# RMSNorm of the next phase inside the input-embedding loop, and a five-slot weight ring, in an eight-core encoder trunk

## The chip, the cores and the metric

The kernel runs on all eight NeuronCores of one Trainium2 chip. Each core computes one of the eight batch elements; the cores exchange nothing. The metric is the device time of the slowest core, in microseconds (us).

A core has five engines that are coupled by semaphores alone: TensorE (PE in the profile) multiplies matrices from SBUF into the eight PSUM banks, VectorE (DVE) and ScalarE (ACT) do elementwise work, GpSimd (POOL) issues DMAs here and little else, SyncE (SP) issues DMAs. Every engine works its own instructions off in program order.

## What is computed

Four layers over a residual stream `h` of 2048 tokens by 1024 channels for each core. Two layers (A) are chunked gated MLPs, two (B) are stick-breaking attention with shared K and V, made once after layer 1.

```python
h = x
for i in range(4):
    hn = rmsnorm(h, norm_g[i])
    if i < 2:
        mix = gmlp_mixer(hn, ...)        # z = hn @ w_in (1024 x 6144); ... @ w_out (2048 x 1024)
    else:
        if k_sh is None:
            kv = rmsnorm(h, kv_norm_g) @ w_kv
        mix = (stick_breaking(q, k_sh, v_sh) * silu(gate)) @ b_w_out[j]   # q, gate = hn @ b_w_in[j]
    h = h + mix
    h = h + sigmoid(h @ ple_gate_w[i]) * (p[i] @ ple_w[i])                # per-layer input embedding
return rmsnorm(h, final_g)
```

The last line of the loop is what the change touches, together with the `rmsnorm` that follows it.

## The kernel before

**Tiling.** `H` (16 tiles of 128 tokens by 1024 channels, float32) stays in SBUF for the whole program. Work goes in halves of 1024 tokens, that is eight tiles: layer 0 half 0, layer 0 half 1, layer 1 half 0, and so on; after layer 1 come two K/V phases (`phase_kv`), one for each half. Every phase needs `HT`, the transposed bfloat16 copy of eight normalized tiles; there is one `HT`, so a half's copy is overwritten by the next one.

**A phase.** `phase_norm` (L423) loads the gain vector into `GB` (L424, queue SP), which is the same memory as `TAA`. Then for each of eight tiles DVE writes `HN` = `H` x `RS` x `GB` (L429), PE transposes it in eight small matmuls (L448) and ACT copies the result to `HT` (L450). The row scales `RS` come from `norm_stats`, which a phase runs ahead for the other half; so they are there before they are needed, with few exceptions. Then the layer's own matmuls run: for A layers L493 (the v columns), the spatial gate L533/L539, L562/L567 (u and gate columns) and the output projection L599 with the residual add L603; for B layers L721 (q and gate), the attention steps, and the output projection L909 with the residual add L913. The output projection has two passes over the eight tiles, one for each half of the output columns (`dc`). In the second pass each tile is also cast to bfloat16 (L437, DVE), transposed (L448) and copied to `HT` (L450): this is the input of the embedding's gate.

**The embedding, `phase_ple`.** Two passes again, `dc` = 0 and 1, each over eight tiles. A tile of a pass is eight gate matmuls (L633), two matmuls of the embedding (L638), a tanh on ACT into `TAA` (L642), and two DVE instructions, L644 and L648, the second of which updates `H`. `HT` is read by both passes. When both are over, the next phase begins with `phase_norm`; its load of `GB` waits until DVE has read `TAA` for the last time.

**The weight ring.** Weights come as units of 128 x 2048 values (read as float32, written as bfloat16, 512 KB each) by DMAs on POOL's queue. `NSLOT` = 4 slots lie in `RING`; A layers have two more in `X`. `ring_begin` marks all earlier units as done (`keep=1` spares one), `ring_next` takes the next unit, `ring_prefetch` issues loads as far as slots are marked free. A load's issue waits on POOL until PE has read the slot's old unit. The embedding has five units: two of gate weights for `dc` = 0 (PW0, PW1), one of embedding weights for both passes (PW2), two of gate weights for `dc` = 1 (PW3, PW4). The output projection of an A layer has eight units (WO0 to WO7), four for each pass; that of a B layer four (BO0 to BO3), two for each pass.

**Order.** The program is recorded by `Sched` as it is written: each engine's order is the order of the calls in the code. `Sched.op` adds the waits that reads and writes of the named regions need.

Of the kernel before, what the change touches and what calls it, by code (L numbers as in the profile page):

```python
# [1 line left out]
OPT = "sp"  # L2
# [5 lines left out]
F32 = mybir.dt.float32  # L8
# [181 lines left out]
VOFF = {}  # L190
# [28 lines left out]
def build(layers=(0, 1, 2, 3), final=True, dbg=False):  # L219
# [63 lines left out]
    SML = sb("SML", [128, 64], F32)  # L283
    ST8 = sb("ST8", [128, 192], F32)
    ST = SML[:, 0:24]
# [27 lines left out]
    rLP = [Reg(), Reg(), Reg()]; rAT = [Reg(), Reg()]  # L313
    rLNG = Reg(); rLNB = Reg(); rVH2 = [Reg(), Reg()]; rWST = Reg(); rBS = Reg(); rBSHL = Reg(); rBSR = Reg()
    rST = Reg(); rMV = Reg(); rSV = Reg()
    rST8 = [Reg() for _ in range(8)]
    rX = [Reg(f"X{i}") for i in range(8)]
    rPS = [Reg(f"ps{i}") for i in range(8)]
    rY = Reg("Y")

    cnt = {"ta": 0, "tb": 0, "hn": 0, "bank": 0, "lp": 0, "at": 0}

# [129 lines left out]
    def phase_A(l, hf):  # L452
# [154 lines left out]
        if l == 0 and hf == 0:  # L607
            dump("H1", H[:, 0:8192], rH[0:8])
        phase_ple(l, hf)

    def phase_ple(l, hf):
        if "p" not in OPT:
            for ii in range(8):
                ple_prep_tile(hf, ii)
        base = widx["PW", l]
        sw = None
        wp = None
        for dc in range(2):
# [70 lines left out]
    def phase_B(l, hf):  # L689
        if True:  # L690
# [209 lines left out]
            for dc in range(2):  # L900
# [3 lines left out]
                for ii in range(8):  # L904
# [74 lines left out]
```

How the kernel before makes its waits and increments, by code:

```python
    def _wait(self, eng, toks):  # L59
        best = {}
        for t in toks:
            if t is None:
                continue
            assert t.sem is not None, f"unresolved token from {t.eng} needed by {eng}"
            key = t.sem
            if key not in best or best[key].val < t.val:
                best[key] = t
        for key, t in best.items():
            if self.seen[eng].get(key, 0) >= t.val:
                continue
            self.E[eng].wait_ge(t.sem, t.val)
            self.seen[eng][key] = t.val
# [23 lines left out]
    def op(self, eng, fn, reads=(), writes=(), signal=True):  # L96
        self._wait(eng, self._deps(eng, reads, writes))
        inst = fn(self.E[eng])
        tok = Tok(eng)
        if signal:
            if self.cnt[eng] >= SEM_CHUNK:
                self._newsem(eng)
            self.cnt[eng] += 1
            inst.then_inc(self.sems[eng], 1)
            tok.sem = self.sems[eng]
            tok.val = self.cnt[eng]
            for p in self.pending[eng]:
                p.sem = tok.sem
                p.val = tok.val
            self.pending[eng] = []
        else:
            self.pending[eng].append(tok)
        self._mark(tok, reads, writes)
        return tok
# [1 line left out]
    def dma(self, q, out, in_, semname, reads=(), writes=()):  # L116
# [3 lines left out]
        ent = self.dsem[semname]  # L120
        ent[1] += 16
        self.E[q].dma_start(out=out, in_=in_).then_inc(ent[0], 16)
        tok = Tok("dma:" + semname)
```

## Time and profile before

| | us |
|---|---|
| median of 3 runs | 3573.12 |
| range of these runs | 3570.70 to 3576.19 |
| the profiled execution, its own time | 3588.44 |
| its span, first to last instruction, slowest core (core 5) | 3587.4 |
| spans of the eight cores | 3553.2 to 3587.4 |

| engine | busy us | share of the span |
|---|---|---|
| PE | 2611.7 | 73% |
| DVE | 1959.7 | 55% |
| ACT | 1747.1 | 49% |
| POOL | 131.1 | 4% |

The shares are of the whole span and hide that the stages have different limits. The places of interest are found in the chain of work that ended last: the profile follows it back from the last instruction, at each step to what released it. A DMA in that chain is time in which the core waited for a transfer. In the timeline a bracket tells how long an engine was idle before an instruction and what released it.

### The profile page before, as it was taken

The page shows a single profiled execution, that of the slowest core. Times are in us where ns is not written, and L with a number is a line of the kernel's source. Part 1 is how long each engine was busy: PE and PEld are TensorE (multiplying, and loading weights), DVE is VectorE, ACT ScalarE, POOL GpSimd, SP SyncE. Part 2 cuts the span into 40 slices and gives each one's busy share as a digit, 9 for nine tenths or more (in the row PEclk, how much of TensorE's full clock was granted, in tenths as well). Part 3 has the DMA queues.
Part 4 walks back from the last instruction along what each step waited for, and adds up shares of the span by engine and source line. Part 5 has one row for each costly group of instructions (what it writes and reads, how often), then busy time and mean ns, then how long its engine had stood idle before and what let it go on. Part 6 is the DMA issues. An engine that isn't in the chain of part 4 may idle for free.

```text
span 3587.4 us, 44009 instructions; the slowest of 8 cores (3553.2 to 3587.4 us)
## 1 busy us (share of the span) xinstructions
PE 2611.7 (73%) x11968; PEld 1142.0 (32%) x11968; DVE 1959.7 (55%) x3224; ACT 1747.1 (49%) x3147; POOL 131.1 (4%) x247
## 2 busy tenths in 40 slices
PE   2789786978698778978877756676667676667671
PEld 1334332433243333434333322222323332222230
DVE  1444246525643455333488457777458845777743
ACT  3442145314531254114266348888446635888832
POOL 0000000000000000000000000000000000000000
PEclk9769986998699888998888979999979897999996
DMA  6214332423133222423311220000221021000022
GB/s 168 47 32 69 54 64 53 76 41 69 36 65 59 59 48 48 77 45 61 53 19 19 36 41 13 13 7 6 36 41 24 13 46 31 13 13 13 1 36 105
DMA packets 43309, 157.10 MB, mean 44 GB/s; under 512 B 4672, under 2 KB 4800, under 8 KB 42560
## 3 DMA queue, kind: packets, MB, share of 16 engines
q0 software_dynamic: 36016, 126.50, 20.7%
q1 hardware_dynamic: 7056, 27.79, 2.2%
q8 instruction: 106, 1.74, 0.2%
q14 instruction: 131, 1.07, 0.1%
HBM read 272.37 MB, written 8.39 MB: 78 GB/s over the span
## 4 chain that ended last, share of the span: by engine, by line
PE 51%; DVE 18%; ACT 12%; issue 12%; DMA 5%; SPq 1%; DVEq 1%; ACTq 0%; POOL 0%; POOLq 0%
PE ps L562 6%; PE ps L567 6%; PE ps L599 6%; PE ps L493 6%; PE ps L633 6%; ACT EE L802 3%; PE ps L721 3%; PE ps L909 3%; DVE TAA L745 3%; DVE LSUM L835 3%; ACT LP L804 3%; PE ps L448 2%; DMA RING<-wts 2%; PE ps L789 2%; DMA TAA<-vecs 2%
## 5 line engine op out<-in xcount | busy, mean ns | idle before, releaser
L450 ACT COPY HT<-ps 128x1024 bf16<-128x1024 bf16 x144 | 145.6, 1012 | 622.1 <-PE ps L448 619.2
L835 DVE TENSOR_TENSOR LSUM<-LSUM,LP 128x512 f32<-128x512 f32 (+3 forms) x576 | 335.7, 583 | 152.1 <-ACT LP L804 136.8
L804 ACT ACTIVATE LP<-EE 128x512 bf16<-128x512 f32 (+3 forms) x640 | 362.0, 566 | 92.5 <-ACT EE L802 2.1
L802 ACT ACTIVATE EE<-ps 128x512 f32<-128x512 f32 (+3 forms) x640 | 338.4, 529 | 104.2 <-PE ps L793 68.4
L825 ACT ACTIVATE AT<-ps 128x512 bf16<-128x512 f32 (+3 forms) x640 | 331.6, 518 | 109.8 <-PE ps L816 106.7
L816 PE MATMUL ps<-LSUMB,CST 128*128 128x512 bf16 (+2 forms) x576 | 220.5, 383 | 202.0 <-DVE LSUMB L838 199.5
L811 PE MATMUL ps<-LP,CST 128*128 128x512 bf16 (+3 forms) x640 | 235.8, 368 | 154.9 <-ACT LP L804 153.0
L448 PE MATMUL ps<-CST,HN 128*128 128x128 bf16 x1152 | 120.5, 268 | 300.9 <-DVE HN L429 182.3
L721 PE MATMUL ps<-HT,RING 128*128 128x512 bf16 x1024 | 306.7, 413 | 0.3 <-ACT HT L450 0.2
L838 DVE CAST LSUMB<-LSUM 128x512 bf16<-128x512 f32 x576 | 246.2, 427 | 100.4 <-DVE LSUM L835 77.9
L789 PE MATMUL ps<-PT,X 128*128 128x512 bf16 (+3 forms) x640 | 238.8, 374 | 54.6 <-DVE PT L726 37.4
L745 DVE RECIPROCAL TAA<-TAA 128x128 f32<-128x128 f32 x256 | 242.2, 946 | 6.8
L847 PE MATMUL ps<-AT,X 128*128 128x512 bf16 (+3 forms) x640 | 239.3, 374 | 7.9 <-ACT AT L825 6.6
L633 PE MATMUL ps<-RING,HT 128*128 128x512 bf16 x864 | 213.8, 388 | 18.4 <-DMA RING<-wts 18.4
L577 DVE SCALAR_TENSOR_TENSOR TBB<-TAA,ps 128x512 bf16<-128x512 f32 x128 | 88.0, 687 | 227.0 <-ACT TAA L575 227.0
L448 PEld LDWEIGHTS ps<-CST,HN 128*128 128x128 bf16 x1152 | 92.1, 120 | 352.8 <-issue 352.8
L599 PE MATMUL ps<-RING,X 128*128 128x512 bf16 x736 | 180.4, 397 | 23.5 <-DMA RING<-wts 23.5
L122 POOL DMA_DIRECT2D RING<-wts x184 | 98.3, 537 | 2525.2 <-PE ps L789 920.5
L642 ACT ACTIVATE TAA<-ps 128x512 f32<-128x512 f32 x128 | 76.4, 597 | 233.7 <-PE ps L633 233.7
L603 DVE TENSOR_TENSOR H<-H,ps 128x512 f32<-128x512 f32 x64 | 44.0, 687 | 256.0 <-PE ps L599 256.0
L493 PE MATMUL ps<-RING,HT 128*128 128x512 bf16 x736 | 178.1, 399 | 0.0
L644 DVE SCALAR_TENSOR_TENSOR TAA<-TAA,ps 128x512 f32<-128x512 f32 x128 | 88.1, 688 | 156.4 <-ACT TAA L642 83.9
(104 smaller groups left out, 3908.1 us busy)
## 6 DMA issues: line engine op xcount, KB each, us to landing
RING<-wts POOLq DMA_DIRECT2D x184, 512.0 KB, 5.3
X<-wts POOLq DMA_DIRECT2D x48, 512.0 KB, 6.2
H<-x SPq DMA_DIRECT2D x16, 512.0 KB, 29.4
y<-H SPq DMA_DIRECT2D x16, 512.0 KB, 2.6
TAA<-vecs SPq DMA_DIRECT2D x11, 512.0 KB, 8.7
OGT<-vecs SPq DMA_DIRECT2D x4, 1024.0 KB, 17.4
PT<-pT POOLq DMA_DIRECT2D x8, 512.0 KB, 7.5
X<-vecs SPq DMA_DIRECT2D x2, 512.0 KB, 14.7
```

The source lines that it names most:

```text
L448: sc.op("pe", lambda e: e.transpose(out=pv[:, k, :], in_=src[:, k * 128:(k + 1) * 128], identity=IDENT), reads=[rsrc, rCST], writes=[rPS[b ...
L493: sc.op("pe", lambda e: e.matmul(PS[b][:, :], lhsT=HT3[:, k, ii * 128:(ii + 1) * 128], rhs=slot3(s_, 4)[:, k % 4, :], start=(k == 0), stop ...
L599: sc.op("pe", lambda e: e.matmul(PS[b][:, :], lhsT=X3[:, ii, k * 128:(k + 1) * 128], rhs=slot3(s_, 4)[:, k % 4, :], start=(k == 0), stop=( ...
L633: sc.op("pe", lambda e: e.matmul(PS[bg][:, :], lhsT=HT3[:, k, ii * 128:(ii + 1) * 128], rhs=slot3(s_, 4)[:, k % 4, :], start=(k == 0), sto ...
L721: sc.op("pe", lambda e: e.matmul(PS[b][:, :], lhsT=w3[:, k, co:co + 128], rhs=HT3[:, k, st * 512:(st + 1) * 512], start=(k == 0), stop=(k ...
L745: sc.op("dve", lambda e: e.reciprocal(out=TA[ta][:, sl_], in_=TA[ta][:, sl_]), reads=[rTA[ta]], writes=[rTA[ta]])
L789: sc.op("pe", lambda e: e.matmul(Z[:, cs], lhsT=KT3[:, hd, kb * 128:(kb + 1) * 128], rhs=QT[qb][:, qs], start=True, stop=not diag, skip_gr ...
L802: sc.op("act", lambda e: e.activation(out=EE[:, cs], in_=PS[zb][:, cs], func=AF.Exp), reads=[rPS[zb]], writes=[rEE])
L804: sc.op("act", lambda e: e.activation(out=LP[lb][:, cs], in_=EE[:, cs], func=AF.Ln, bias=1.0), reads=[rEE], writes=[rLP[lb]])
L825: sc.op("act", lambda e: e.activation(out=AT[ab][:, cs], in_=PS[zb][:, cs], func=AF.Exp), reads=[rPS[zb]], writes=[rAT[ab]])
L835: sc.op("dve", lambda e: e.tensor_tensor(out=LSUM[:, cs], in0=LSUM[:, cs], in1=LP[lb][:, cs], op=ALU.add), reads=[rLS, rLP[lb]], writes=[rLS])
L838: sc.op("dve", lambda e: e.tensor_copy(out=LSUMB[k_][:, :], in_=LSUM[:, :]), reads=[rLS], writes=[rLSB[k_]])
```

## The change

1. `phase_ple` is one pass over the tiles, with `dc` as the inner loop. All five units are taken at its start, so all must be in slots at once; `NSLOT` becomes 5 (seven slots in A layers).
2. After both `dc` of a tile, `norm_apply_tile` makes the next phase's normalized and transposed tile at once: DVE L621, transposes L451, copy L453. `HT` of the tile was read for the last time by the tile's gate matmuls. The phase that follows finds it done (`pre_applied`) and skips `phase_norm`. This is so for seven of the ten norms: into half 1 of each of the four layers, into layer 1 half 0, into the first K/V phase, into layer 3 half 0. The first norm, the one of the second K/V phase and the one of layer 2 half 0 stay as they were; the embedding of layer 3 half 1 has no norm behind it.
3. `GB` is loaded at the start of `phase_ple`. The tanh results go to `EE` and `LSUM` in turn, since `TAA` now holds the gain.
4. To pay for the fifth slot, `LP` has two buffers, not three, and `ST8` (statistics of the layernorm) lies in `TBB`.

```diff
-NSLOT = 4
+NSLOT = 5
...
+    ST8 = TBB[:, 0:384].bitcast(F32)
...
-    LP = [sb(f"LP{i}", [128, NQ], BF16) for i in range(3)]
+    LP = [sb(f"LP{i}", [128, NQ], BF16) for i in range(2)]
...
     def phase_norm(goff, hf):
+        if pre_applied["key"] == (goff, hf):
+            pre_applied["key"] = None
+            return
...
+    def norm_apply_tile(hf2, ii):
+        i = hf2 * 8 + ii
+        hb = nxt("hn", 2)
+        sc.op("dve", lambda e: e.scalar_tensor_tensor(out=HN[hb][:, :], in0=H3[:, i, :], scalar=RS[:, i:i + 1],
+                                                       in1=GB[:, :], op0=ALU.mult, op1=ALU.mult),
+              reads=[rH[i], rRS] + rGBL, writes=[rHN[hb]])
+        transpose_tile(HN[hb], rHN[hb], 8, None, [rHT[ii]], HT3[:, :, ii * 128:(ii + 1) * 128])
+
+    def phase_ple(l, hf, nxt_norm=None):
         base = widx["PW", l]
...
-        for dc in range(2):
-            if dc == 0:
-                ring_begin()
-                sg = [ring_next(base + 0), ring_next(base + 1)]
-                sw = ring_next(base + 2)
...
-            else:
-                ring_begin(keep=1)
-                sg = [ring_next(base + 3), ring_next(base + 4)]
-            ring_prefetch(3)
-            for ii in range(8):
-                i = hf * 8 + ii
+        ring_begin()
+        un = [ring_next(base + i) for i in range(5)]
+        ring_prefetch()
...
+        if nxt_norm is not None:
+            goff2, hf2 = nxt_norm
+            norm_stats(hf2)
+            sc.dma("sp", GB[:, :], vecs_d[:, goff2:goff2 + 1024], "gb", writes=rGBL)
+        for ii in range(8):
+            i = hf * 8 + ii
+            for dc in range(2):
+                sg = un[0:2] if dc == 0 else un[3:5]
...
-                sc.op("act", lambda e: e.activation(out=TA[ta][:, :], in_=PS[bg][:, :], func=AF.Tanh, scale=0.5),
-                      reads=[rPS[bg]], writes=[rTA[ta]])
+                tp_ = nxt("ptmp", 2)
+                T_, rT_ = PTMP[tp_], rPTMP[tp_]
+                sc.op("act", lambda e: e.activation(out=T_[:, :], in_=PS[bg][:, :], func=AF.Tanh, scale=0.5),
+                      reads=[rPS[bg]], writes=[rT_])
...
+            if nxt_norm is not None:
+                norm_apply_tile(nxt_norm[1], ii)
```

PE's order from the end of the embedding of layer 0 half 0 into the next phase, before. A row is line, operation, what is written and read, and the shape; L633 is a gate matmul, L638 one of the embedding, L448 a transpose, L493 the next phase's first weight matmul.

```order
L633 MATMUL ps6<-X,HT 128x512 x4
L633 MATMUL ps6<-RING,HT 128x512 x4
L638 MATMUL ps7<-X,PT 128x512 x2
L448 MATMUL ps0<-CST,HN0 128x128 x8
L448 MATMUL ps1<-CST,HN1 128x128 x8
L448 MATMUL ps2<-CST,HN0 128x128 x8
...
L448 MATMUL ps7<-CST,HN1 128x128 x8
L493 MATMUL ps0<-RING,HT 128x512 x8
L493 MATMUL ps1<-RING,HT 128x512 x8
```

All eight groups of transposes stand behind the sixteen tile passes of the embedding. The same engine after the change, first the tiles 6 and 7 of the same embedding and then the next phase; L644 is the gate, L649 the embedding, L451 a transpose, L496 the next phase.

```order
L649 MATMUL ps1<-X,PT 128x512 x2
L451 MATMUL ps2<-CST,HN0 128x128 x8
L644 MATMUL ps3<-RING,HT 128x512 x4
L644 MATMUL ps3<-X,HT 128x512 x4
L649 MATMUL ps4<-X,PT 128x512 x2
L644 MATMUL ps5<-RING,HT 128x512 x8
L649 MATMUL ps6<-X,PT 128x512 x2
L451 MATMUL ps7<-CST,HN1 128x128 x8
L496 MATMUL ps0<-RING,HT 128x512 x8
```

A tile's transposes now stand between its own last matmul and the next tile's first.

DVE's order at the end of the same embedding, before; L644 and L648 are the two instructions of a tile pass, L429 the norm.

```order
L644 SCALAR_TENSOR_TENSOR TAA<-TAA,ps5 128x512
L648 SCALAR_TENSOR_TENSOR H<-TAA,H 128x512
L644 SCALAR_TENSOR_TENSOR TAA<-TAA,ps7 128x512
L648 SCALAR_TENSOR_TENSOR H<-TAA,H 128x512
L429 SCALAR_TENSOR_TENSOR HN0<-H,RS,TAA 128x1024
L429 SCALAR_TENSOR_TENSOR HN1<-H,RS,TAA 128x1024
```

DVE's order in tiles 0 and 1 of the embedding after the change; L656 and L660 are the tile's two instructions for each `dc`, L621 the norm of a tile of the next half.

```order
L656 SCALAR_TENSOR_TENSOR EE<-EE,ps1 128x512
L660 SCALAR_TENSOR_TENSOR H<-EE,H 128x512
L656 SCALAR_TENSOR_TENSOR LSUM<-LSUM,ps3 128x512
L660 SCALAR_TENSOR_TENSOR H<-LSUM,H 128x512
L621 SCALAR_TENSOR_TENSOR HN0<-H,RS,TAA 128x1024
L656 SCALAR_TENSOR_TENSOR EE<-EE,ps6 128x512
```

The norm of a tile stands behind the four instructions of the same tile, though it reads another half of `H` and needs none of them.

POOL's loads from the last unit before the output projection's weights of layer 0 half 0 are complete to the next phase's, before. They are WO4, the embedding input `PT`, WO5, WO6, WO7, PW0, PW1, PW2, PW3; a wait on `s_pe_1` is one until PE is through with the slot's old unit.

```order
L122 DMA X<-wts 128x2048 [waits d_ring4,s_pe_1]
L122 DMA PT<-pT 128x2x1024
L122 DMA X<-wts 128x2048 [waits d_ring5,s_pe_1]
L122 DMA RING<-wts 128x2048 [waits d_ring0,s_pe_1]
L122 DMA RING<-wts 128x2048 [waits d_ring1]
L122 DMA RING<-wts 128x2048 [waits d_ring2]
L122 DMA RING<-wts 128x2048 [waits d_ring3]
L122 DMA X<-wts 128x2048 [waits d_ring4,s_pe_1]
L122 DMA X<-wts 128x2048 [waits d_ring5]
```

After the change the same stretch is WO5, `PT`, WO6, WO7, PW0, PW1, PW2, PW3, PW4, and then the next phase's first units.

```order
L122 DMA RING<-wts 128x2048 [waits d_ring1,s_pe_1]
L122 DMA PT<-pT 128x2x1024
L122 DMA RING<-wts 128x2048 [waits d_ring2,s_pe_1]
L122 DMA RING<-wts 128x2048 [waits d_ring3,s_pe_1]
L122 DMA RING<-wts 128x2048 [waits d_ring4]
L122 DMA X<-wts 128x2048 [waits d_ring5]
L122 DMA X<-wts 128x2048 [waits d_ring6]
L122 DMA RING<-wts 128x2048 [waits d_ring0,s_pe_1]
L122 DMA RING<-wts 128x2048 [waits d_ring1]
```

WO6 has moved ahead of the end of the projection's first pass, WO7 not; PW3 and PW4 still wait until PE is through with the projection's second pass.

## Rows read from the trace of the kernel before

**Rows 1.** The page of the profile: its span, and the chain that ended last.

```profile
span 3587.4 us, 44009 instructions; the slowest of 8 cores (3553.2 to 3587.4 us)
...
PE 51%; DVE 18%; ACT 12%; issue 12%; DMA 5%; SPq 1%; DVEq 1%; ACTq 0%; POOL 0%; POOLq 0%
```

**Rows 2.** Stretches from an embedding's first gate matmul to the next phase's first.

```profile
core 5: us, PE busy (x) PEld busy (x) DVE busy (x) ACT busy (x) POOL busy (x), PEclk, DMA share, GB/s
421.24:484.17 62.93, 44.07 (x227) 22.06 (x225) 32.03 (x40) 17.37 (x24) 3.11 (x6) 0.81 0.47 84
...
1190.10:1248.96 58.86, 42.68 (x227) 21.77 (x225) 32.01 (x40) 17.31 (x24) 3.02 (x6) 0.85 0.45 89
...
2041.72:2108.07 66.35, 45.33 (x228) 22.17 (x226) 31.97 (x40) 19.01 (x26) 2.64 (x5) 0.80 0.31 63
...
sum 440.85, PE 309.13 PEld 154.14 DVE 230.22 ACT 125.66 POOL 19.80; mean PE 44.16 PEld 22.02 DVE 32.89 ACT 17.95 POOL 2.83
```

**Rows 3.** The chain, end of layer 2 half 0: start us, us, what.

```profile
2082.77 0.43 PE ps L638 x2
2083.20 1.74 PE ps L633 x8
...
2085.08 0.61 ACT TAA L642
...
2085.85 0.70 DVE TAA L644
...
2086.64 0.70 DVE H L648
...
2087.41 8.74 DMA TAA<-vecs
...
2096.25 1.30 DVE HN L429
2097.55 0.24 issue
```

**Rows 4.** The chain, last tile of layer 2's output projection.

```profile
2036.15 0.70 DVE HN L437
...
2037.10 0.61 PE ps L448 x8
2037.70 1.74 PE ps L909 x8
...
2039.97 5.13 DMA RING<-wts
```

**Rows 5.** Timeline of PE after waits: start us, us, what, count [idle before].

```profile
426.56 1.01 PE L638 MATMUL ps<-X,PT 128*128 128x512 bf16 x2 [3.43 <-DMA X<-wts]
427.36 2.85 PE L633 MATMUL ps<-RING,HT 128*128 128x512 bf16 x8
430.04 0.59 PE L638 MATMUL ps<-X,PT 128*128 128x512 bf16 x2
...
2066.58 1.86 PE L633 MATMUL ps<-RING,HT 128*128 128x512 bf16 x4 [4.67 <-DMA RING<-wts]
...
2072.25 1.89 PE L633 MATMUL ps<-RING,HT 128*128 128x512 bf16 x8
```

**Rows 6.** Timeline of PE, second pass of two A output projections, tile 0.

```profile
369.75 1.87 PE L599 MATMUL ps<-RING,X 128*128 128x512 bf16 x4 [5.85 <-DMA RING<-wts]
373.73 1.87 PE L599 MATMUL ps<-RING,X 128*128 128x512 bf16 x4 [2.11 <-DMA RING<-wts]
...
1517.44 1.22 PE L599 MATMUL ps<-RING,X 128*128 128x512 bf16 x4 [4.08 <-DMA RING<-wts]
1520.06 1.87 PE L599 MATMUL ps<-X 128*128 128x512 bf16 x4 [1.40 <-DMA X<-wts]
```

**Rows 7.** The chain: the embedding's first missing unit, layer 0 half 0.

```profile
419.49 6.83 DMA X<-wts
```

**Rows 8.** Last embedding, first to last matmul, columns as in rows 2.

```profile
3477.09:3519.87 42.78, 36.35 (x163) 15.76 (x160) 20.69 (x30) 11.53 (x18) 0.53 (x1) 0.96 0.20 36
```

More of the change, by code:

```diff
@@ L283, in build @@
     SML = sb("SML", [128, 64], F32)
-    ST8 = sb("ST8", [128, 192], F32)
     ST = SML[:, 0:24]
@@ L307, in build @@
     rTB = [Reg() for _ in range(4)]
+    rST8 = [rTB[0]] * 8
     rGBL = rTA
@@ L312, in build @@
     rLS = Reg(); rLSB = [Reg(), Reg()]; rEE = Reg()
-    rLP = [Reg(), Reg(), Reg()]; rAT = [Reg(), Reg()]
+    rLP = [Reg(), Reg()]; rAT = [Reg(), Reg()]
     rLNG = Reg(); rLNB = Reg(); rVH2 = [Reg(), Reg()]; rWST = Reg(); rBS = Reg(); rBSHL = Reg(); rBSR = Reg()
     rST = Reg(); rMV = Reg(); rSV = Reg()
-    rST8 = [Reg() for _ in range(8)]
     rX = [Reg(f"X{i}") for i in range(8)]
@@ L319, in build @@
     rY = Reg("Y")
-    cnt = {"ta": 0, "tb": 0, "hn": 0, "bank": 0, "lp": 0, "at": 0}
+    cnt = {"ta": 0, "tb": 0, "hn": 0, "bank": 0, "lp": 0, "at": 0, "ptmp": 0}
     def nxt(key, n):
@@ L608, in phase_A @@
             dump("H1", H[:, 0:8192], rH[0:8])
-        phase_ple(l, hf)
-    def phase_ple(l, hf):
-        if "p" not in OPT:
-            for ii in range(8):
-                ple_prep_tile(hf, ii)
-        base = widx["PW", l]
-        sw = None
-        wp = None
-        for dc in range(2):
-            if dc == 0:
-                ring_begin()
-                sg = [ring_next(base + 0), ring_next(base + 1)]
-                sw = ring_next(base + 2)
-                wp = slot_ap[sw].rearrange("p (d k c) -> p d k c", d=2, k=2)
-            else:
-                ring_begin(keep=1)
-                sg = [ring_next(base + 3), ring_next(base + 4)]
-            ring_prefetch(3)
-            for ii in range(8):
-                i = hf * 8 + ii
+        phase_ple(l, hf, next_norm_of.get((l, hf)))
+    pre_applied = {"key": None}
+    PTMP = [EE, LSUM]
+    rPTMP = [rEE, rLS]
+    def norm_apply_tile(hf2, ii):
[6 more added lines that the diff above has]
+    def phase_ple(l, hf, nxt_norm=None):
+        base = widx["PW", l]
+        ring_begin()
+        un = [ring_next(base + i) for i in range(5)]
+        ring_prefetch()
+        sw = un[2]
+        wp = slot_ap[sw].rearrange("p (d k c) -> p d k c", d=2, k=2)
+        if nxt_norm is not None:
[6 more added lines that the diff above has]
+                sg = un[0:2] if dc == 0 else un[3:5]
                 bg = bank()
@@ L640, in phase_ple @@
                           reads=rPTL + [rSLOT[sw]], writes=[rPS[bp]], signal=(k == 1))
-                ta = nxt("ta", 2)
-                sc.op("act", lambda e: e.activation(out=TA[ta][:, :], in_=PS[bg][:, :], func=AF.Tanh, scale=0.5),
-                      reads=[rPS[bg]], writes=[rTA[ta]])
-                sc.op("dve", lambda e: e.scalar_tensor_tensor(out=TA[ta][:, :], in0=TA[ta][:, :], scalar=1.0, in1=PS[bp][:, :],
+                tp_ = nxt("ptmp", 2)
+                T_, rT_ = PTMP[tp_], rPTMP[tp_]
+                sc.op("act", lambda e: e.activation(out=T_[:, :], in_=PS[bg][:, :], func=AF.Tanh, scale=0.5),
+                      reads=[rPS[bg]], writes=[rT_])
+                sc.op("dve", lambda e: e.scalar_tensor_tensor(out=T_[:, :], in0=T_[:, :], scalar=1.0, in1=PS[bp][:, :],
                                                                op0=ALU.add, op1=ALU.mult),
-                      reads=[rTA[ta], rPS[bp]], writes=[rTA[ta]])
+                      reads=[rT_, rPS[bp]], writes=[rT_])
                 hv = H3[:, i, dc * 512:(dc + 1) * 512]
-                sc.op("dve", lambda e: e.scalar_tensor_tensor(out=hv, in0=TA[ta][:, :], scalar=0.5, in1=hv, op0=ALU.mult, op1=ALU.add),
-                      reads=[rTA[ta], rH[i]], writes=[rH[i]])
+                sc.op("dve", lambda e: e.scalar_tensor_tensor(out=hv, in0=T_[:, :], scalar=0.5, in1=hv, op0=ALU.mult, op1=ALU.add),
+                      reads=[rT_, rH[i]], writes=[rH[i]])
+            if nxt_norm is not None:
+                norm_apply_tile(nxt_norm[1], ii)
         stats_ready[hf] = False
+        pre_applied["key"] = nxt_norm
     KT3 = X[:, 0:16384].rearrange("p (h t) -> p h t", t=S)
@@ L799, in emit_ELP @@
                 zb = s["zb"]
-                lb = nxt("lp", 3)
+                lb = nxt("lp", 2)
                 s["lb"] = lb
@@ L916, in phase_B @@
                         ple_prep_tile(hf, ii)
-        phase_ple(l, hf)
+        phase_ple(l, hf, next_norm_of.get((l, hf)))
     def phase_final():
@@ L936, in store_raw @@
             sc.dma("sp", y_d[i * 128:(i + 1) * 128, :], H3[:, i, :], "y", reads=[rH[i]], writes=[rY])
+    next_norm_of = {}
+    for l in layers:
+        next_norm_of[(l, 0)] = (VOFF[f"ng{l}"], 1)
+        if l == 1 and (2 in layers or 3 in layers):
+            next_norm_of[(l, 1)] = (VOFF["kvg"], 0)
+        elif (l + 1) in layers and l != 1:
+            next_norm_of[(l, 1)] = (VOFF[f"ng{l + 1}"], 0)
     plan()
```

## The prediction

> **What bounds the kernel now.** The page comes first: of the chain that ended last, PE is 51%, DVE 18%, DMA 5% [rows 1]. So the span is made of stages in which PE sets the pace and of joints in which it waits. The joints to look at are those between an embedding and the next phase. The table of stretches gives them from the embedding's first gate matmul to the next phase's first: 58.9 to 66.4 us each, 440.85 us for the seven that the change fuses [rows 2].
>
> The chain shows what such a stretch is made of [rows 3]. A tile pass is 1.74 + 0.43 = 2.17 us of matmuls, sixteen passes are 34.7 us, and during them PE does not wait for ACT or DVE. Behind the last pass stand tanh, two DVE instructions, the 8.74 us load of the gain vector (it could not start earlier, since `GB` is `TAA`), and eight tiles of norm and transposes. From 2084.94 (end of the last gate group) to 2108.07 [rows 2, 3] that is 23.1 us, and this joint is what the change wants to remove. The rest of a stretch is waits for weight units: PW2 for 5.13 us after the projection's end in a B layer [rows 4], 6.83 us once in layer 0 [rows 7], and PE idle for 4.67 us before PW3 or PW4 in a B layer [rows 5].
>
> **What the change removes.** The gain's load goes to the start of the embedding and is hidden: SP has nothing else queued, `TAA` is free by then, and the loop lasts several times its 8.74 us. The eight norms leave the joint. Their work remains, 1.30 us of DVE and 0.61 us of transposes for a tile.
>
> **What it adds: a chain in every tile.** The order of the engines decides this part. On DVE a tile's norm stands behind the same tile's four instructions; on PE its transposes stand behind the tile's last matmul and before the next tile's first. The order gives PE nothing to do in between. From the end of the second gate group the steps are [rows 3]: 2.40 us until the second DVE instruction is over (2084.94 to 2086.64 + 0.70), 0.10 hand-over, 1.30 norm, 0.24 until the transposes start; 4.04 us in all, of which PE fills 0.43 with the embedding's matmuls. PE idles 3.6 us in each tile. Before, the same three steps of ACT and DVE ran beneath the next pass. A tile is then 0.61 transposes [rows 4] + 1.74 + 0.43 + 1.74 + 4.04 = 8.56 us at full clock, eight tiles 68.5 us. That alone is above all of the 58.9 us stretches, in which this work was done in two separate blocks.
>
> **The clock.** Matmuls of 512 columns run in 0.217 us where the granted clock is the full 2.4 GHz (1.74 for eight). After PE had been idle for 3.43 us they ran at half of it: ten matmuls took 3.48 us (426.56 to 430.04) and not 2.17, so 1.3 us more; after 4.67 us, sixteen took 5.67 us (2066.58 to 2072.25) and not 3.47, 2.2 us more [rows 5]. After the 1.85 us gap around the cast of a projection tile, matmuls came at full speed [rows 4]. The new gap of 3.6 us is nearer to 3.43 than to either other one, and it returns in every tile; the twenty matmuls of a tile are long enough to win the clock back, so it is lost again each time. The bounds of the price are nothing and 2.2 us a tile. I take 1.6 us, between the two rows, nearer to 1.3 because its gap is the nearer one, and for seven tiles of eight since the first tile comes out of a busy stretch: 11.2 us for a loop.
>
> The Trainium skill, TensorE: Matmul & The Clock Gate, section on HAM oscillation, warns of just this shape: bursts of matmuls with a wait between them, where the clock falls in the wait of every iteration and the price is paid each time. By that rule a loop is 79.7 us, by a clock that holds 68.5; rows 5 agree with the rule for gaps of this size.
>
> **The units.** All five must be there in tile 0. PW0 to PW2 are, PW3 and PW4 are issued when PE is through with the projection, at 0.5 us behind its end. In the B layer the first unit of such a pair let PE go at 2045.34, that is 3.6 us after the gate's start at 2041.72 (2039.97 + 5.13, and some 0.24) [rows 2, 4]; in layer 0 at 426.56, 5.3 us after 421.24 [rows 2, 5, 7]. The second unit of a pair arrives 2.6 to 4.0 us behind the first (1517.44 and 1520.06; 369.75 and 373.73) [rows 6]. PE wants PW4 at 2.17 + 0.87 = 3.0 us. So it waits between 3.2 and 6.3 us in tile 0; I take 4.2, nearer to the B layers' 3.2, which have the quieter queue. The next phase's first unit in a B layer goes into PW0's slot, which tile 7 leaves free after its first gate group, over 6 us before the loop's end; with 5.13 us to land it is no new wait.
>
> A fused stretch is 68.5 + 11.2 + 4.2 = 83.9 us; seven are 587, against 440.85: **+146 us**.
>
> **What the fifth slot gives.** In the second pass of an A projection two units come late, WO6 and WO7. WO6 is now loaded ahead, WO7 lands when WO6 did. Saved is the distance of the two, 3.98 us and 2.62 us in the two places shown, out of four [rows 6]: four times some 3.1, **−12 us**. It could be more by the clock that stays up, or less if WO7 alone is no faster.
>
> **The last embedding** has no norm. It took 42.78 us with two waits [rows 8]. Now sixteen passes of 2.17, one wait of 4.2, and 1.6 of slow clock are 40.5: **−2 us**.
>
> **At nothing.** `LP` with two buffers: an `LP` buffer is rewritten after ACT's two activations and the step before have gone by, and its readers on PE and DVE are ones that ACT's next exponential waits for anyway; cover is that wait, and without it a step could pay part of its DVE add. `ST8` in `TBB`: its users are done before `TBB` is written. One more unit at the program's start competes with the loads of `H`: 0 to 3 us, taken as 0. After the loop, the next phase begins with a cold PE in both kernels.
>
> **Sum.** 146 − 12 − 2 = +132 us (+131.5 before rounding). The profiled execution took 3588.44 us, so 3720 in its own terms; it lies 15.3 us above the median of the runs, 3573.12. On the median: **3704 us**, 3.7% slower.
>
> **Rivals.**
> - *The clock holds.* The 3.6 us gap could fall so that the clock survives it. Then a stretch is 72.7 us, seven are 509, +68 − 14 = +54: 3627 us. For it: gaps of 1.85 us are harmless [rows 4]. Against: 3.43 us already was not [rows 5]. In between lie loops in which it falls in one tile and not in the next, 3640 to 3690.
> - *The clock never comes back.* Then twenty matmuls are 8.5 us and a tile is 1.0 + 3.4 + 0.85 + 3.4 + 4.04 = 12.7 us; a stretch 106 us, seven 742, +301 − 14: 3860 us. Against: in rows 5 it was back after ten to sixteen matmuls, and a tile has twenty.
> - *The other side: the chain is hidden.* If the transposes waited without holding up the next tile's matmuls, a stretch would be 34.7 + 8 x 0.61 + 4.2 = 43.8 us, seven 307, −134 − 14: 3425 us. The place is the end of each tile on PE. The break-even: 440.85 + 14 is 65.0 us a stretch, less 4.2 is 60.8, so a tile of 7.6 us; the wait for the norm would have to shrink by 1 us even at full clock. Against: the order on PE; in the projection's second pass, which has the same form, the next tile's matmuls (2037.70) came only behind the transposes (2037.10), which waited for the cast (2036.15) [rows 4]. The Trainium skill says in the same page, section on what happens when a matmul is issued, that only weight loads are pulled ahead and matmuls stay in program order; this row agrees.
> - *It doesn't do what it says*, that is, a key does not match and the norms are made twice or not fused: the order shows seven fused groups, so this has next to no chance.
>
> **How the numbers follow.** The clock falls in most tiles: 0.80, centre 3704, its own range 3650 to 3750 by the price of a drop (1.3 to 2.2 us) and the wait for units (3.2 to 6.3). The clock holds: 0.10. It never comes back: 0.04. The chain is hidden: 0.05, of which 0.01 end near no change. The range of 3640 to 3750 leaves out the last three and the tails of the first, some 2 in 10. A measurement of this kernel can tell 0.2%, 7 us, from no change. Slower by more than that: 0.95; within it: 0.01; faster: 0.04.
>
> **What would show it.** In the changed kernel's timeline a tile of the fused loop should have L451 behind a wait of 3.2 to 3.8 us for the norm L621, a period near 10 us, and gate matmuls at half clock behind most waits; the granted clock of these stretches should fall from 0.80 to 0.85 to about 0.75. The fused stretches should add up to 560 to 620 us. The load of `TAA` should be gone from the chain, and an A projection's second pass should have one wait for `RING` instead of two. I am wrong if the period is under 9 us (the clock holds), if PE's wait in front of L451 is short (DVE's order is not what it seems), or if the attention steps have grown (`LP`).

## The result: 3.0% slower

| | before | after |
|---|---|---|
| median of the runs, us | 3574.66 (10 runs) | 3681.82 (9 runs) |
| ratio of the undisturbed runs, 95% interval | | 1.0303, 1.0290 to 1.0316 |
| span of the profiled execution, slowest core, us | 3587.4 | 3680.8 |
| spans of the eight cores, us | 3553.2 to 3587.4 | 3666.1 to 3680.8 |

Some executions of this program, of either kernel, are disturbed and take up to 8% longer; ratios go by the others, and where a median would hold disturbed runs the ratio is given instead, with the fastest run. The forecast was 3704 us with a range of 3640 to 3750.

The page of the changed kernel: the span, the chain by engine, and the group of the transposes (count, busy us, mean ns, idle us before them and the releaser).

```profile
span 3680.8 us, 43875 instructions; the slowest of 8 cores (3666.1 to 3680.8 us)
...
PE 51%; DVE 19%; ACT 13%; issue 12%; DMA 3%; SPq 1%; DVEq 1%; ACTq 0%; POOL 0%; POOLq 0%
...
L451 PE MATMUL ps<-CST,HN 128*128 128x128 bf16 x1152 | 103.3, 242 | 386.2 <-DVE HN L621 184.6
```

DMA's share of the chain fell from 5% [rows 1] to 3%: the gain's load is gone, as meant. In its place stand 184.6 us in which PE waited for `HN` of L621. There are 7 x 8 = 56 fused tiles, so 3.3 us each.

The slowest core is now core 1, so the two kernels are compared on core 1. Its fused stretches, from the embedding's first gate matmul to the next phase's first; first the kernel before, then after (columns as in rows 2).

```profile
1165.63:1224.27 58.64, 42.75 (x228) 21.73 (x226) 31.99 (x40) 17.39 (x24) 3.11 (x6) 0.84 0.45 89
...
2560.34:2625.57 65.23, 44.21 (x227) 22.00 (x225) 32.02 (x40) 18.56 (x25) 2.63 (x5) 0.84 0.32 64
...
sum 436.52, PE 307.38 PEld 153.73 DVE 230.21 ACT 125.77 POOL 19.86; mean PE 43.91 PEld 21.96 DVE 32.89 ACT 17.97 POOL 2.84
```

```profile
1201.84:1281.67 79.83, 51.08 (x227) 21.45 (x225) 31.64 (x40) 17.65 (x24) 3.11 (x6) 0.85 0.19 37
...
2651.38:2732.28 80.90, 51.53 (x227) 22.17 (x225) 31.65 (x40) 18.93 (x25) 2.63 (x5) 0.83 0.13 23
...
sum 566.57, PE 357.82 PEld 152.76 DVE 221.94 ACT 127.41 POOL 19.69; mean PE 51.12 PEld 21.82 DVE 31.71 ACT 18.20 POOL 2.81
```

PE, DVE and ACT do nearly the same work in both. PE's busy time grows by 50 us for the same number of matmuls, since many of them run at half clock; the rest of the 130 us is waiting.

The other stretches that the prediction speaks of, core 1, before: start of the program to the first v-column matmul, the first of the four A output projections, the last embedding.

```profile
0.00:79.83 79.83, 7.88 (x64) 6.25 (x65) 16.38 (x22) 17.65 (x25) 4.56 (x12) 1.00 0.74 189
314.47:401.86 87.39, 64.29 (x322) 28.98 (x321) 18.36 (x27) 7.68 (x8) 4.42 (x9) 0.92 0.23 36
...
3451.10:3493.86 42.76, 36.34 (x163) 15.71 (x160) 20.69 (x30) 11.53 (x18) 0.53 (x1) 0.96 0.19 37
```

The same three after the change.

```profile
0.00:83.35 83.35, 7.89 (x64) 6.26 (x65) 16.38 (x22) 17.65 (x25) 5.09 (x13) 1.00 0.74 187
318.77:400.89 82.12, 62.39 (x321) 28.74 (x321) 18.36 (x27) 7.68 (x8) 4.40 (x9) 0.96 0.27 45
...
3572.58:3612.62 40.04, 36.70 (x163) 15.83 (x160) 20.69 (x30) 11.54 (x18) 0.00 (x0) 0.96 0.13 26
```

The ledger of core 1, in us:

| where | before | after | difference | forecast |
|---|---|---|---|---|
| seven fused stretches | 436.5 | 566.6 | +130.1 | +146 |
| four A output projections | 339.1 | 326.4 | −12.6 | −12 |
| last embedding | 42.8 | 40.0 | −2.7 | −2 |
| start of the program | 79.8 | 83.4 | +3.5 | 0 |
| sum | | | +118.3 | +132 |
| span of core 1 | 3561.3 | 3680.8 | +119.5 | |

So nothing of size happened outside the places named. The runs' medians are 107 us apart, somewhat less than core 1's two profiled executions.

### The profile page after: what moved, and what is told of

It is laid out like the page before. It is cut to its first block, busy times and chain, and to the rows that moved or that the text cites. A ratio compares the mean times of both kernels' runs of the same rounds, so it can differ in the third digit from the quotient of the medians.

```text
span 3680.8 us, 43875 instructions; the slowest of 8 cores (3666.1 to 3680.8 us)
## 1 busy us (share of the span) xinstructions
PE 2644.4 (72%) x11968; PEld 1137.8 (31%) x11968; DVE 1963.0 (53%) x3224; ACT 1747.0 (47%) x3147; POOL 131.3 (4%) x247
## 3 DMA queue, kind: packets, MB, share of 16 engines
q8 instruction: 106, 1.74, 0.2%
## 4 chain that ended last, share of the span: by engine, by line
PE 51%; DVE 19%; ACT 13%; issue 12%; DMA 3%; SPq 1%; DVEq 1%; ACTq 0%; POOL 0%; POOLq 0%
PE ps L644 7%; PE ps L565 6%; PE ps L570 6%; PE ps L602 6%; PE ps L496 6%; PE ps L736 3%; ACT EE L817 3%; ACT LP L819 3%; PE ps L924 3%; DVE LSUM L850 3%; DVE TAA L760 3%; PE ps L451 2%; DMA RING<-wts 2%; DVE HN L621 2%; DVE LSUMB L853 2%
## 5 line engine op out<-in xcount | busy, mean ns | idle before, releaser
L453 ACT COPY HT<-ps 128x1024 bf16<-128x1024 bf16 x144 | 145.7, 1012 | 715.6 <-PE ps L451 715.5
L451 PE MATMUL ps<-CST,HN 128*128 128x128 bf16 x1152 | 103.3, 242 | 386.2 <-DVE HN L621 184.6
L736 PE MATMUL ps<-HT,RING 128*128 128x512 bf16 x1024 | 309.6, 416 | 0.0
L644 PE MATMUL ps<-RING,HT 128*128 128x512 bf16 x896 | 273.4, 455 | 24.7 <-DMA RING<-wts 24.7
L451 PEld LDWEIGHTS ps<-CST,HN 128*128 128x128 bf16 x1152 | 78.4, 107 | 451.0 <-issue 451.0
L656 DVE SCALAR_TENSOR_TENSOR EE<-EE,ps 128x512 f32<-128x512 f32 x64 | 44.0, 688 | 266.9 <-ACT EE L654 183.2
L565 PE MATMUL ps<-HT,RING 128*128 128x512 bf16 x736 | 178.7, 387 | 0.0
L570 PE MATMUL ps<-HT,RING 128*128 128x512 bf16 x736 | 174.5, 380 | 0.0
```

What stands on the lines that cost most here:

```text
L451: sc.op("pe", lambda e: e.transpose(out=pv[:, k, :], in_=src[:, k * 128:(k + 1) * 128], identity=IDENT), reads=[rsrc, rCST], writes=[rPS[b ...
L565: sc.op("pe", lambda e: e.matmul(PS[bu][:, :], lhsT=w3[:, k, 0:128], rhs=HT3[:, k, st * 512:(st + 1) * 512], start=(k == 0), stop=(k == 7) ...
L570: sc.op("pe", lambda e: e.matmul(PS[bg][:, :], lhsT=w3[:, k, 128:256], rhs=HT3[:, k, st * 512:(st + 1) * 512], start=(k == 0), stop=(k == 7)),
L644: sc.op("pe", lambda e: e.matmul(PS[bg][:, :], lhsT=HT3[:, k, ii * 128:(ii + 1) * 128], rhs=slot3(s_, 4)[:, k % 4, :], start=(k == 0), sto ...
L736: sc.op("pe", lambda e: e.matmul(PS[b][:, :], lhsT=w3[:, k, co:co + 128], rhs=HT3[:, k, st * 512:(st + 1) * 512], start=(k == 0), stop=(k ...
```

## One tile of the fused loop

The chain of the changed kernel in a steady tile of layer 0 half 0 (start us, us, what):

```profile
430.03 1.74 PE ps L644 x8
...
431.91 0.61 ACT LSUM L654
...
432.68 0.70 DVE LSUM L656
...
433.47 0.06 DVE H L660
433.53 0.55 issue
434.08 1.29 DVE HN L621
435.37 0.14 issue
435.50 0.69 PE ps L451 x8
436.20 3.32 PE ps L644 x8
...
439.95 1.74 PE ps L644 x8
```

This is the forecast's chain, step by step [rows 3]: gate group, tanh, two DVE instructions, norm, transposes, and only then the next tile's matmuls. The next tile's first eight take 3.32 us and its second eight 1.74: the clock is at half and comes back within the tile. The period is 9.93 us (transposes at 435.50 and, in the next tile, at 445.43), and 9.92 in most of the others.

The clock does not fall in every tile. Of the 49 tiles of core 1 that follow such a wait within a loop, 42 have slow matmuls and 7, one in each loop, run their first gate group in 1.72 us. The last tile of the same loop is one of these; the timeline of PE:

```profile
475.20 0.61 PE L451 MATMUL ps<-CST,HN 128*128 128x128 bf16 x8 [3.32 <-DVE HN L621]
475.65 1.03 PE L644 MATMUL ps<-RING,HT 128*128 128x512 bf16 x4
...
483.44 0.83 PE L451 MATMUL ps<-CST,HN 128*128 128x128 bf16 x8 [3.31 <-DVE HN L621]
```

The wait is as long as in the other tiles, and the period is 8.24 us (475.20 to 483.44). So the two periods stand side by side in one kernel, and a fallen clock costs 1.7 us a tile.

Tile 0 is different, since it also waits for units. The timeline of PE in layer 2 half 0 (idle before, in brackets):

```profile
2092.95 1.89 PE L644 MATMUL ps<-RING,HT 128*128 128x512 bf16 x8
2094.68 0.59 PE L649 MATMUL ps<-RING,PT 128*128 128x512 bf16 x2
2096.60 1.02 PE L644 MATMUL ps<-RING,HT 128*128 128x512 bf16 x4 [1.32 <-DMA RING<-wts]
2099.05 1.86 PE L644 MATMUL ps<-RING,HT 128*128 128x512 bf16 x4 [1.43 <-DMA RING<-wts]
...
2104.70 1.01 PE L451 MATMUL ps<-CST,HN 128*128 128x128 bf16 x8 [2.93 <-DVE HN L621]
```

PW3 comes 1.3 us late and PW4 another 1.4 us, 2.75 us together. In the seven tiles 0 of core 1 the two waits add up to 6.1, 4.4, 2.6, 2.7, 2.75, 2.9 and 2.7 us.

## The experiments

Two theories. **A**: PE waits in every tile for a norm that stands last in the tile's chain, and loses its clock in that wait; the ring, the early gain and the single pass are not what costs. **B**: something else in the change costs: the five units at once, the smaller `LP`, the single pass, or the mixing of transposes and matmuls as such. All ratios are to the kernel before, timed on the same chip.

**e1, the norm ahead on DVE.** One thing is moved in the changed kernel: `norm_dve` is the norm on DVE, `norm_pe` the transposes and the copy.

```diff
         for ii in range(8):
             i = hf * 8 + ii
+            if nxt_norm is not None:
+                hb_n = norm_dve(nxt_norm[1], ii)
             for dc in range(2):
...
             if nxt_norm is not None:
-                norm_apply_tile(nxt_norm[1], ii)
+                norm_pe(hb_n, ii)
```

> The changed kernel with one thing moved: DVE makes a tile's norm ahead of the tile's four own instructions, not behind them; the transposes stay where they are on PE. Theory A (PE waits in every tile for a norm that stands last in the tile's chain, and loses its clock in that wait): the wait in front of the transposes goes, the clock stays up, a fused stretch is 16 x 2.17 + 8 x 0.44 + some 4.2 for the late units = 43 us and not 81, so about 3682 - 7 x 38 = 3415 us, a ratio of about 0.955 to before. Theory B (the loss comes from the five units that must be there at once, from the smaller LP or from mixing transposes with matmuls): the order on DVE changes nothing, 3640 to 3690 us.

Measured: ratio 0.9571 (0.9552 to 0.9590); the fastest run 3414.6 us. The timeline of core 1, layer 0 half 0, a whole tile:

```profile
418.56 1.28 DVE L621 SCALAR_TENSOR_TENSOR HN<-H,RS,TAA 128x1024 bf16<-128x1024 f32 x1
...
419.11 1.89 PE L649 MATMUL ps<-RING,HT 128*128 128x512 bf16 x8
...
420.83 0.59 PE L654 MATMUL ps<-X,PT 128*128 128x512 bf16 x2
...
421.26 0.61 PE L451 MATMUL ps<-CST,HN 128*128 128x128 bf16 x8
...
421.71 1.03 PE L649 MATMUL ps<-RING,HT 128*128 128x512 bf16 x4
```

The norm runs beneath the tile's matmuls, the transposes at 421.26 have no bracket, and the period is 4.77 us (421.26 to 426.03 at the next). The seven stretches of core 1 add up to this, against 566.57:

```profile
sum 304.06, PE 275.58 PEld 135.99 DVE 207.83 ACT 134.69 POOL 14.18; mean PE 39.37 PEld 19.43 DVE 29.69 ACT 19.24 POOL 2.03
```

The position of one DVE instruction decides over 262 us in these stretches. B's suspects are all still in this kernel, and it is 4.3% faster than the one before.

**e2, the gap filled.** The changed kernel with work of no use in PE's gap.

```diff
+NDUM = 12
...
             if nxt_norm is not None:
+                bd = bank()
+                for k in range(NDUM):
+                    sc.op("pe", lambda e: e.matmul(PS[bd][:, :], lhsT=HT3[:, k % 8, ii * 128:(ii + 1) * 128],
+                                                    rhs=wp[:, 0, k % 2, :], start=(k == 0), stop=(k == NDUM - 1)),
...
                 norm_apply_tile(nxt_norm[1], ii)
```

> The changed kernel with twelve matmuls of 512 columns added on PE in each fused tile between its last matmul and the transposes; their result is never read, so they do no useful work. At full clock they take 2.6 us and fit into the 3.3 us that PE waits there. Theory A (1.5 us of each 9.9 us tile are the price of the fallen clock): the clock holds in the loops, a tile is 8.4 us, 7 x 8 x 1.5 = 84 us less, about 3600 us, ratio about 1.007. Rival (the clock is no part of it, or falls for another reason): added work changes nothing or costs time, 3680 us or more, ratio 1.03 or above.

Measured: 3609.8 us, ratio 1.0112 (1.0094 to 1.0129). PE of core 0 in a tile (L666 are the added matmuls), and the sum of its seven stretches:

```profile
431.72 1.03 PE L645 MATMUL ps<-RING,HT 128*128 128x512 bf16 x4
432.59 1.03 PE L645 MATMUL ps<-X,HT 128*128 128x512 bf16 x4
...
436.26 2.54 PE L666 MATMUL ps<-X,HT 128*128 128x512 bf16 x11
439.52 0.61 PE L452 MATMUL ps<-CST,HN 128*128 128x128 bf16 x8 [0.72 <-DVE HN L622]
```

```profile
sum 487.92, PE 428.27 PEld 197.35 DVE 221.90 ACT 127.40 POOL 14.26; mean PE 61.18 PEld 28.19 DVE 31.70 ACT 18.20 POOL 2.04
```

With 672 matmuls more the kernel is 72 us faster than the changed one (68 us by the two ratios). The first gate matmuls of a tile come at full speed, eight in 1.73 us (431.72 to 433.45), in all 49 tiles behind a wait and on all eight cores, and the period is 8.24 us (431.28 to 439.52). So the chain alone gives 8.24 us a tile, as in six of the seven fast tiles of the changed kernel (8.59 in the other), and the fallen clock adds 1.68; 42 such tiles are 71 us. Holding the clock up in the loops takes back about two thirds of the 107 us lost against the kernel before. That kernel has slow matmuls of its own, so the 72 us are what a steady clock is worth in the changed kernel, and not simply a part of the 107. What is left is still 1.1% slower than before: the wait for the chain alone is enough for a loss.

**e3, the ring alone.** The kernel before with `NSLOT = 5`, two `LP` buffers and `ST8` in `TBB`; `phase_ple` as it was.

```diff
-NSLOT = 4
+NSLOT = 5
...
-    LP = [sb(f"LP{i}", [128, NQ], BF16) for i in range(3)]
+    LP = [sb(f"LP{i}", [128, NQ], BF16) for i in range(2)]
```

> The kernel before with the fifth slot alone (and the two buffers of LP and the place of ST8 that pay for it); the embedding is as before. Theory A: one wait less in each A output projection, 12 us less, 3562 us, ratio 0.9965. Theory B (the smaller LP slows the attention steps, or the ring is part of the loss): at or above the time before, ratio 1.000 to 1.02.

Measured: ratio 0.9854 (0.9837 to 0.9871), 53 us less than before. Neither theory said so. The page's group of gate matmuls shows why: no idle time at all in front of them, while the kernel before had 18.4 us there and more in front of L638.

```profile
L633 PE MATMUL ps<-RING,HT 128*128 128x512 bf16 x896 | 214.3, 379 | 0.0
```

```profile
1996.08:2053.45 57.37, 42.79 (x227) 21.77 (x225) 31.92 (x40) 18.99 (x26) 2.64 (x5) 0.84 0.37 73
...
3408.11:3442.81 34.70, 34.70 (x163) 15.55 (x160) 20.53 (x30) 11.54 (x18) 0.00 (x0) 1.00 0.15 30
```

In two passes PW3 and PW4 are wanted 17 us after the embedding begins, and PW2 now arrives before it begins. A B layer's stretch falls from 65.3 to 57.4 us, the last embedding from 42.8 to the bare 34.7. Of core 1's 51 us, 38 are in the seven stretches (436.5 to 398.4), 8 in the last embedding and 11 in the four A projections (339.1 to 328.1); some 6 are lost again elsewhere, 2.4 of them at the start of the program (79.83 to 82.21). I had counted the slot's worth in the projections alone. The changed kernel has that slot too, but takes all five units at once and so brings waits back: its last embedding is 40.0 us, not 34.7.

**e4, one pass with the norms behind it.** The changed kernel with the gain early and all norms and transposes after the loop.

```diff
-            if nxt_norm is not None:
-                norm_apply_tile(nxt_norm[1], ii)
+        if nxt_norm is not None:
+            for ii in range(8):
+                norm_apply_tile(nxt_norm[1], ii)
```

> The changed kernel with the one-pass embedding and the early load of the gain, but all eight norms and transposes behind the loop instead of in it. Theory A (the norm's place in the loop makes the loss): a stretch is 34.7 for the matmuls, some 5.8 for the late units and the clock after them, 2.4 for the tail of the last tile and 11.8 for the norms, 54.7 us; seven are 183 us below the 566 us of the changed kernel, about 3500 us, ratio 0.98. Theory B (the one pass with five units at once makes the loss): a stretch stays near 80 us or gets longer, 3670 us or more.

Measured: ratio 0.9784 (0.9760 to 0.9807); the fastest run 3491.3 us. The seven stretches of core 1:

```profile
sum 368.56, PE 306.44 PEld 151.53 DVE 224.27 ACT 125.36 POOL 19.84; mean PE 43.78 PEld 21.65 DVE 32.04 ACT 17.91 POOL 2.83
```

52.7 us a stretch for 54.7 expected. The change without its fusion gains 2.2%; the fusion, as placed, turns that into a loss of 3.0%. B's single pass is cleared as the cause of the loss, though not of every cost (see e5).

**e5, the early gain alone.** The kernel before with the tanh results in `EE` and `LSUM` and the load of `GB` at the embedding's start.

```diff
+        if nxt_norm is not None:
+            sc.dma("sp", GB[:, :], vecs_d[:, nxt_norm[0]:nxt_norm[0] + 1024], "gb", writes=rGBL)
...
-                sc.op("act", lambda e: e.activation(out=TA[ta][:, :], in_=PS[bg][:, :], func=AF.Tanh, scale=0.5),
+                sc.op("act", lambda e: e.activation(out=T_[:, :], in_=PS[bg][:, :], func=AF.Tanh, scale=0.5),
```

> The kernel before with one thing: the tanh results go to EE and LSUM, and the gain of the next norm is loaded at the start of the embedding. Two passes, norm behind them, four slots, as before. Theory A (the load's 8.7 us stand alone in the joint): 7 x 8.7 = 61 us less, 3510 us, ratio 0.983. Rival (something else is late there, or the tanh buffers cost): less than 30 us, ratio above 0.992.

Measured: ratio 0.9837 (0.9813 to 0.9860), 58 us for 61 expected. The seven stretches of core 1 get 54 us shorter (436.5 to 382.5), 7 to 10 us each but for the second, 4.0. So the load stood alone in the joint, and little came late in its place.

e3 and e5 together price the single pass. The slot alone is worth 53 us and the early gain alone 58, 111 if they add up; e4 has both, and the single pass, and gains 77. The 34 us between are an estimate of what taking all five units at once costs. The stretches agree in the main: by e3 and e5 one should take 436.5 less 38 and 54, over seven 49.2 us, and e4's takes 52.7; its last embedding has the units at once too. The change against the kernel before is then −53 and −58 for its good parts, +34 for the single pass and, from e4 to the changed kernel, some +185 for the norm in each tile as it is placed. Theory A had the single pass at nothing; it was not nothing, and it was not the loss.

**e6, e1 in two passes.** `phase_ple` of e1 with `dc` as the outer loop again; norm and transposes of a tile stand in the second pass.

```diff
+        for dc in range(2):
+            ...
+            for ii in range(8):
+                if dc == 1 and nxt_norm is not None:
+                    hb_n = norm_dve(nxt_norm[1], ii)
+                ...
+                if dc == 1 and nxt_norm is not None:
+                    norm_pe(hb_n, ii)
```

> The kernel of e1 (norm first on DVE) with the embedding's two passes back: PW3 and PW4 are wanted only in the second pass, and the norms and transposes stand in that pass. Theory A (taking all five units at once costs a wait for PW3 and PW4 in each embedding): that wait goes, a fused stretch is 17.4 + 8 x 2.9 (DVE sets the pace in the second pass) + 1 = 42 us and not 44.7, the last embedding 34.7 and not 38 to 40: 20 to 25 us less than e1, about 3392 us, ratio 0.950. Rival (the waits for units are hidden or come back elsewhere, or DVE's pace in the second pass eats it): as e1, 3415 us or more, ratio 0.957.

Measured: 3416.5 us, ratio 0.9560 (0.9542 to 0.9579): as e1. The stretches of core 1:

```profile
1116.27:1158.74 42.47, 38.75 (x227) 18.76 (x225) 29.95 (x38) 17.61 (x24) 1.45 (x3) 1.00 0.38 74
...
sum 299.43, PE 272.78 PEld 131.39 DVE 210.81 ACT 127.47 POOL 10.78; mean PE 38.97 PEld 18.77 DVE 30.12 ACT 18.21 POOL 1.54
```

4.6 us less than e1 in the sum, where theory A expected some 19. The stretch shown is 42.5 us, so the second pass is 25 us, 3.1 us a tile where PE needs 2.6: the second pass has all eight norms, and PE waits for `HN` of L621 there, 24.5 us in all. The rival came out in the total. The waits for units are gone from all eight embeddings, and the last one takes 34.7 us and not 40.0; but e1's stretches had been shorter than thought (43.4 us each for 44.7), DVE takes part of the gain, and e1 was 8 us faster than e6 in the four attention stretches of layers 2 and 3, from the first q matmul to the output projection (1319.0 and 1326.9 us, 1328.2 in the kernel before), for which no cause was traced. Once the norm is placed well, the single pass is a fair trade.

**e7, the same cure one stage earlier.** As e6, and in the output projections' second pass a tile's transposes stand behind the next tile's matmuls (`prep_flush` makes those that are pending).

```diff
     def ple_prep_tile(hf, ii):
         i = hf * 8 + ii
+        prep_flush()
         hb = nxt("hn", 2)
         sc.op("dve", lambda e: e.tensor_copy(out=HN[hb][:, :], in_=H3[:, i, :]), ...)
-        transpose_tile(HN[hb], rHN[hb], 8, None, [rHT[ii]], HT3[:, :, ii * 128:(ii + 1) * 128])
+        prep_pend.append((hb, ii))
```

> As e6, and the same cure in the second pass of the output projections: a tile's transposes stand behind the next tile's matmuls, so PE does not wait for the residual add and the cast. Theory A (the wait in front of in-line transposes is paid in full wherever it stands): a tile of that pass falls from 5.8 to 3.9 us in A layers and from 4.1 to 2.2 in B layers, 8 x 8 x 1.9 = 120 us less than e6, about 3272 us, ratio 0.916. Rival (other limits take over, DVE or the weight units): under 60 us less.

Measured: ratio 0.9212 (0.9157 to 0.9267), the fastest run 3283.0 us. The group of transposes on its page:

```profile
L459 PE MATMUL ps<-CST,HN 128*128 128x128 bf16 x1152 | 96.7, 232 | 112.2 <-DVE HN L432 86.2
```

The wait for the cast is gone from the list of releasers. Of what is left, 86.2 us belong to the norms that are not fused; on core 1, 22.6 us are for L629, the fused norm in the embedding's second pass. The profiled execution is 132 us shorter than that of e6 (3282.0 and 3414.5), 2.1 us in each of the 64 tiles for 1.9 expected. The wait in front of in-line transposes had stood in the kernel before too, 115.9 us by its page's view of waits, in 64 tiles.

**e8, the two norms left over.** As e7, with the norms of the second K/V phase and of layer 2 half 0 made in the last pass of the V projections, norm first on DVE.

```diff
     def phase_kv(hf):
         phase_norm(VOFF["kvg"], hf)
+        nx = (VOFF["kvg"], 1) if hf == 0 else ((VOFF["ng2"], 0) if 2 in layers else None)
+        if nx is not None:
+            norm_stats(nx[1])
+            if hf == 1:
+                sc.dma("sp", GB[:, :], vecs_d[:, nx[0]:nx[0] + 1024], "gb", writes=rGBL)
...
+                if fuse:
+                    hb_n = norm_dve(nx[1], ii)
...
+                if fuse:
+                    norm_pe(hb_n, ii)
```

> As e7, and the two norms that the change leaves alone (second K/V phase, layer 2 half 0) are made in the last pass of the V projections in the same way. Two joints of some 12 to 20 us go: 20 to 35 us less than e7, about 3245 us, ratio 0.908.

Measured: ratio 0.9139 (0.9121 to 0.9157), the fastest run 3265.4 us. That is 18 us less than e7's fastest and not the 20 to 35 expected. On core 1 the two joints, from the last V matmul to the next phase's first, go from 14.6 and 12.3 us in e7 to 0.7 and 1.4, so 25 us go; but the matmuls of the two K/V phases, with norms and transposes among them now, take 9 us longer. What e7's cure does is seen in this kernel too. PE in an A projection's second pass, core 1:

```profile
363.35 3.62 PE L610 MATMUL ps<-RING,X 128*128 128x512 bf16 x16
366.80 0.61 PE L459 MATMUL ps<-CST,HN 128*128 128x128 bf16 x8
```

3.9 us a tile, and no bracket. This version is 8.6% faster than the kernel before and 11.3% faster than the changed one (0.9139 / 1.0303 = 0.887).

## Why the prediction was right, and where it was off

- **The chain in every tile**: right, and the cause of the loss. The forecast had 4.04 us from the second gate group to the transposes; in the tile shown it is 3.73 (431.77 to 435.50). The two steps that were too long are the hand-over from L660 to the norm and the one to PE. The norm reads another half of `H` and needs nothing of L660, so DVE starts it 0.61 us after L660's start and not 0.79, as between the dependent L656 and L660; and PE starts 0.14 after it, not 0.24. PE's idle time is 3.3 us, forecast 3.6.
- **The clock**: right in kind and size. The forecast was 1.6 us in each of seven tiles, 11.2 us a loop; measured were 9.92 − 8.24 = 1.68 us in six tiles of a loop, 10.1 us, and e2 against the changed kernel gives 72 us in all. The section on HAM oscillation of the Trainium skill's page TensorE: Matmul & The Clock Gate, which the prediction set against a clock that holds, has the clock fall in the wait of every iteration. It is borne out in 42 of 49 tiles; in the other seven the clock held over the same wait of 3.3 us, which the prediction had only as a case between its rivals. What the prediction said of the granted clock was wrong: it stayed at 0.81 to 0.87 in the stretches and did not fall to 0.75. Before, the share at half clock was the joint and what followed it; now it is spread over the tiles. Average clock over a stretch could not have told the two kernels apart; the durations of single groups did.
- **The units**: the wait was forecast at 3.2 to 6.3 us in tile 0 and taken as 4.2. Five of the seven were below that range, at 2.6 to 2.9 us; the mean is 3.4. A stretch came to 80.9 us on core 1 instead of 83.9: that, times seven, is 21 us less by rounded means (587 and 566.6), of which the shorter chain is 7 x 8 x 0.3 = 17 us.
- **The fifth slot in the A projections**: −12.6 for −12. One wait for a unit is left of two, as forecast. But the four places gave 5.3, 1.0, 3.4 and 3.0 us where the forecast took some 3.1 for each (the two rows that it shows average 3.3), so part of the agreement is luck; in the second the one wait left, 5.5 us, is longer than the first of the two had been, 5.1. **The last embedding**: −2.7 for −2. But the slot's worth in the embedding, had its two passes stayed, was not seen (e3).
- **LP at nothing**: right, though the waits moved. The four attention stretches of core 1 take 1328.2 us before and 1327.6 after. The first of the long attention stretches (layer 2 half 1), core 1, before and after:

```profile
2081.44:2513.45 432.01, 290.41 (x1201) 108.70 (x1201) 317.63 (x577) 358.72 (x708) 4.95 (x9) 0.95 0.06 10
```

```profile
2173.03:2604.49 431.46, 294.95 (x1204) 109.96 (x1202) 317.64 (x577) 358.14 (x708) 5.27 (x10) 0.94 0.09 15
```

And in the view of waits of the changed kernel (us in total, times, longest) a new one has come, for the missing buffer, while ACT's wait in front of `AT` fell from the 106.6 us of core 1 before:

```profile
ACT LP L819 <- DVE LSUM L850: 66.3, 32, 9.6
...
ACT AT L840 <- PE ps L831: 36.9, 74, 0.8
```

  ACT waits for `LP` where it would have waited for `AT` a moment later.
- **The start at nothing**: off by 3.5 us. The chain of core 1 waits there for a load into `X`, which starts at 38.47 us and takes 21.90 before, and starts at 39.84 and takes 24.06 after. Every run with the seventh unit has it: on core 1 the start takes 81.6 to 84.2 us in the eight kernels with five slots and 79.8 and 79.6 in the two with four.

- **The rivals**: the clock did not hold, but e2 made it hold, and came out at 3610 us where that rival had 3627. The other side, the chain hidden, was put at 3425 us and held to be barred by PE's order. e1 reached 3415 without touching PE's order: DVE's order alone had to change. The break-even of 7.6 us a tile holds up: e2 has 8.24 us and is 40 us slower than the kernel before, 0.7 us for each of 56 tiles, so an estimate from it is 7.5 us. The way to get below it was not the one that I looked at.

## What to carry over

When work is fused into a loop, ask of each engine not only whether it has room but where in its queue the new instruction stands: an operation that needs nothing of its tile belongs ahead of the tile's dependent instructions, or its consumer one tile later. The price of a wait on TensorE that comes back in every iteration is the wait and the slow matmuls behind it; here the second was worth some 70 us of a loss of 107. A deeper ring is worth what the moment of need allows: taking all units of a stage at its start gave back, by the estimate above, 34 of the 53 us that the added slot alone had won.

## What was not expected of the hardware

- More matmuls made the kernel faster: 672 added ones of 512 columns took 72 us off, since PE's gap shrank from 3.3 to 0.72 us and the granted clock of the stretches rose to 0.98 to 1.00 on core 0 (0.93 to 1.00 over all cores).
- The same wait did not always cost the clock: of 49 waits of 2.9 to 3.7 us in the loops of core 1, 42 were followed by matmuls at half clock and 7 were not.
- Two DVE instructions with no dependency between them overlap: 1024-element norms started 0.61 us after the start of a 0.70 us instruction, against 0.79 us for a dependent one.
- The clock's loss doesn't show in a mean: 0.82 to 0.84 before and 0.81 to 0.87 after over the same stretches.
